# Attention with selected blocks and a window: two factors in one scaling operation

## The reference

```python
ss = jnp.where(dsel >= 0, ss - sl[..., None, None] * dsel, NEG)
ps = jax.nn.softmax(ss.reshape(B, G, R, T, -1), axis=-1).reshape(ss.shape)
o_sel = jnp.einsum('bgrtns,bgtnsd->bgrtd', ps.astype(vb.dtype), vb)
...
pw = jax.nn.softmax(sw, axis=-1)
o_win = jnp.einsum('bgrts,bgsd->bgrtd', pw.astype(vwb.dtype), vwb)
...
gt = jax.nn.sigmoid(gates.reshape(B, S, 3, G, R).transpose(2, 0, 3, 4, 1))[..., None]
o = gt[0] * o_cmp + gt[1] * o_sel + gt[2] * o_win
```

## Time and profile before

| | |
|---|---|
| median of three runs | 3860.39 us (3858.7 to 3864.57) |
| the profiled execution | 3864.79 us, span 3863.0 us |
| mean granted clock of TensorE | 0.946 of 2.4 GHz |
| TensorE (PE) busy in the span | 3528.5 us, 91% |
| VectorE (DVE) busy | 1776.0 us, 46% |
| ScalarE (ACT) busy | 869.9 us, 23% |
| GpSimd (POOL) busy | 1030.7 us, 27% |
| attention stage | 925 to 1290 us from the span's start |

### The profile page before, as it was taken

How to read it: one execution, slowest core, us unless ns; L and a number is a source line. 1 busy time by engine, 2 the same in 40 slices (tenths; PEclk the granted TensorE clock), 3 DMA queues, 4 the chain that set the end, 5 groups by cost and what they waited for, 6 DMA issues and landing times. The chain is left out here.

```text
span 3863.0 us, 55754 instructions
## 1 busy us (share of the span) xinstructions
PE 3528.5 (91%) x23230; PEld 2909.7 (75%) x23230; DVE 1776.0 (46%) x2725; ACT 869.9 (23%) x1260; POOL 1030.7 (27%) x491
## 2 busy tenths in 40 slices
PE   5999999989999898999999889959896899999997
PEld 4878777767777676888888767748784778888886
DVE  4762555423877734555555636134443322223233
ACT  2012122122434203111111220235431121111112
POOL 3332333333210234121212054122212332122221
PEclk7999999998999998999999989969997899999998
DMA  3453334333000312322222046221002111111111
GB/s 92 137 179 116 110 99 118 104 111 102 8 8 1 113 46 89 109 93 69 72 82 76 30 153 150 89 77 36 19 3 93 55 44 44 55 43 54 38 49 44
DMA packets 310711, 290.79 MB, mean 75 GB/s; under 512 B 21454, under 2 KB 276992, under 8 KB 309304
## 3 DMA queue, kind: packets, MB, share of 16 engines
q1 hardware_dynamic: 283738, 205.62, 18.2%
q10 hardware_dynamic: 26482, 82.06, 5.6%
q0 software_dynamic: 288, 0.20, 0.1%
HBM read 224.26 MB, written 63.57 MB: 75 GB/s over the span
## 5 line engine op out<-in xcount | busy, mean ns | idle before, releaser
L713 POOL TENSOR_TENSOR ffn_wlo<-ffn_raw,ffn_whi 128x1024 fp32r<-128x1024 f32 x88 | 211.4, 2404 | 1067.3 <-ACT ffn_whi L901 1012.9
L203 PE MATMUL up<-h_hi,ffn_whi 128*128 128x512 f32 x1408 | 439.6, 394 | 21.3 <-POOL h_lo L404 20.9
L203 PE MATMUL up<-h_lo,ffn_whi 128*128 128x512 f32 x1408 | 436.2, 391 | 0.0
L203 PE MATMUL up<-h_hi,ffn_wlo 128*128 128x512 f32 x1408 | 435.4, 390 | 0.0
L192 POOL TENSOR_TENSOR whi<-raw,ones 128x1024 fp32r<-128x1024 f32 (+1 forms) x83 | 155.3, 1872 | 754.9 <-PE acc L1409 460.9
L203 PEld LDWEIGHTS up<-h_hi,ffn_whi 128*128 128x128 f32 x1408 | 263.4, 189 | 79.2 <-POOL h_lo L404 14.4
L203 PEld LDWEIGHTS up<-h_lo,ffn_whi 128*128 128x128 f32 x1408 | 265.9, 189 | 56.2
L203 PEld LDWEIGHTS up<-h_hi,ffn_wlo 128*128 128x128 f32 x1408 | 265.7, 189 | 56.1
L1409 PE MATMUL acc<-h_hi,whi 128*128 128x512 f32 x816 | 273.6, 417 | 8.3 <-POOL h_lo L404 8.3
L804 DVE TENSOR_TENSOR ffn_prod<-ffn_act,up 128x1024 f32<-128x1024 f32 x44 | 53.8, 1222 | 465.6 <-PE up L203 460.8
L1409 PE MATMUL acc<-h_lo,whi 128*128 128x512 f32 x816 | 256.6, 396 | 0.0
(11 more groups left out here) (549 smaller groups left out, 6635.7 us busy)
## 6 DMA issues: line engine op xcount, KB each, us to landing
raw<-w_in SPq DMA_DIRECT2D x51, 512.0 KB
projT<-proj_stage ACTq DMA_DIRECT2D x51, 512.0 KB, 2.7
ffn_ada_raw<-w_ada SPq DMA_DIRECT2D x24, 1024.0 KB, 5.0
ffn_raw<-w_up SPq DMA_DIRECT2D x44, 512.0 KB
ffn_draw<-w_down SPq DMA_DIRECT2D x11, 1024.0 KB, 6.9
ffn_raw<-ffn_w_gate SPq DMA_DIRECT2D x22, 512.0 KB
ffn_raw<-ffn_w_up SPq DMA_DIRECT2D x22, 512.0 KB
ffn_draw<-ffn_w_down SPq DMA_DIRECT2D x11, 1024.0 KB, 4.7
```

Source lines behind the costliest of these rows:

```text
L203: last = nc.tensor.matmul(acc[:, t, :], w[:, k, w_cols], x[:, k, t * HALF:(t + 1) * HALF], start=(k == 0 and i == 0), stop=(k == k_tiles - ...
L713: nc.gpsimd.tensor_tensor(w_lo[i][:], raw[i][:], w_hi[i][:], ALU.subtract).then_inc(s[f"up_split{i}"], 1)
```

## The change

The product of inverse sum and gate (L2251) is taken out. The scaling (L2254) takes the inverse sum and the gate as its two factors per query, and multiplies by both. The semaphore `weighted`, which counted the products, becomes `inverted` and counts the reciprocals. The column `small[3:4]` is no longer written. All other engines' programs stay.

```diff
@@ nsa_attend
-    names = both("q_in q_split scores_done max_done exp_done weighted scaled grouped group_copied o_done o_read") + ...
+    names = both("q_in q_split scores_done max_done exp_done inverted scaled grouped group_copied o_done o_read") + ...
@@ weight(j)
                 dve.wait_ge(s[f"exp_done{r}"], j // 2 + 1)
                 dve.wait_ge(s[f"scaled{r}"], j // 2)
-                steps.link(nc.vector.reciprocal(small[r][:, 2:3], small[r][:, 1:2]))
+                nc.vector.reciprocal(small[r][:, 2:3], small[r][:, 1:2]).then_inc(s[f"inverted{r}"], 1)
                 gate = (1 + r) * NSA_H + h
-                nc.vector.tensor_tensor(small[r][:, 3:4], small[r][:, 2:3], N["gates"][:, i, gate:gate + 1], ALU.mult).then_inc(s[f"weighted{r}"], 1)
                 n = tiles(i, r) * P
-                dve.wait_ge(s[f"weighted{r}"], j // 2 + 1)
-                nc.vector.tensor_scalar(prob[r][:, 0:n], prob[r][:, 0:n], small[r][:, 3:4], None, ALU.mult).then_inc(s[f"scaled{r}"], 1)
+                dve.wait_ge(s[f"inverted{r}"], j // 2 + 1)
+                nc.vector.tensor_scalar(prob[r][:, 0:n], prob[r][:, 0:n], small[r][:, 2:3], N["gates"][:, i, gate:gate + 1],
+                                        ALU.mult, ALU.mult).then_inc(s[f"scaled{r}"], 1)
```

More of the change, by code:

```diff
@@ L2091, in nsa_attend @@
     raw, w_hi, w_lo = (x[0][:, 0:4, :] for x in mem.weights)
-    names = both("q_in q_split scores_done max_done exp_done weighted scaled grouped group_copied o_done o_read") + "o_in0 o_in1 o_in2 o_in3 o_in4 o_in5 o_in6 o_in7 vector_step pool_step weight_loaded weight_high weight_split"
+    names = both("q_in q_split scores_done max_done exp_done inverted scaled grouped group_copied o_done o_read") + "o_in0 o_in1 o_in2 o_in3 o_in4 o_in5 o_in6 o_in7 vector_step pool_step weight_loaded weight_high weight_split"
     banks = [(f"sc{r}", [P, S], F32) for r in range(2)] + [(f"{n}{r}", [P, HALF], F32) for n in ("pt", "ob") for r in range(2)]
```

## The result

The changed kernel takes 3822.9 us at the median of five runs (3814.8 to 3825.5), against 3864.6 before in the same measurement (3858.7 to 3869.4). The ratio is 0.9894, interval 0.9879 to 0.9909, so some 41 us faster (35 to 47 by the interval). The direction and the places were forecast.

A forecast was written before the change was run, and what follows sets the result against it. In the attention stage, the tensor engine was taken to lose time to waits for DVE's loop and to its lower clock. Terms of 12 (A), 7 (B) and 6 (C) gave 25 us, so 3835 us, range 3826 to 3843, low end 3824.

The forecast's parts named there:

- second factor: In DVE's scaling, the gate as another factor per partition was to cost 0.06 us per scaling.
- fast form: DVE's faster mode for the scaling, expected to stay; the rival that the second factor costs it had chance 0.09, about 3848.
- net 0.14 us per job: DVE's loop: 0.195 us saved by dropping the product, less 0.06 for the longer scaling.
- Term C: Small row blocks: the shorter loop saves 1.0 us per head; 6 us taken in all, bounds 0 and 11.
- Term A: Head boundaries: tensor engine waits behind GpSimd shrink, as one operation queues instead of two; 12 us, bounds 9.5 to 14.1.
- wait for the copy between: Head boundaries: a wait between two short waits, named in the rival that the clock still falls, without a size.
- my replay: One head boundary reworked with one queueing: the first wait goes, 0.4 us of the second wait's 1.34 stays.
- term B: Tensor engine clock at head boundaries: four of five falls to 1.2 GHz go; 7 us, bounds 0 and 8.5.
- Beyond these jobs the loop is ahead, and the saving is idle time of DVE: Jobs past the small row blocks: the shorter loop was to gain nothing there.
- The clock did not keep falling: Rival at head boundaries: shortened waits still drop the tensor engine's clock; 18 us gain at most, about 3844, chance 0.18.
- The waiting was swallowed: Answers a rival: the scaling meets another GpSimd instruction and the tensor engine waits as long as before; 3854, chance 0.09.
- The slower case: Rival: the scaling takes its slow form and still queues behind GpSimd; 8 us or more slower, about 3869, chance 0.04.

The follow-up runs named there:

- e3: Kernel before the change, with GpSimd's query splitting for heads 2 to 7 left out but for two columns of one operation; 3827.5 us, ratio 0.9924.
- e4: Changed kernel with GpSimd's query splitting for heads 2 to 7 left out but for two columns of one operation; 3820.7 us, ratio 0.9898.
- e1: Kernel before the change, its product kept but written as a scaling by a factor per partition, which does not queue behind GpSimd; 3838.6 us, ratio 0.9944.
- e5: Changed kernel with a second, unused reciprocal ahead of the scaling in every job, making the loop longer without queueing; 3841.4 us, ratio 0.9937.
- e9: Kernel before with its product in the non-queueing form, and GpSimd's splits starting only after the widest selected-branch scaling; 3841.0 us, ratio 0.9940.
- e12: Changed kernel with a second reciprocal only in the six jobs of row blocks 5 to 7 of each head; 3832.0 us, ratio 0.9920.
- e8: Changed kernel measured once more, unchanged; 3822.4 us, ratio 0.9886.
- e10: Kernel before the change, with GpSimd's splits starting only after the widest selected-branch scaling; 3838.0 us, ratio 0.9934.
- e7: Changed kernel with the copies of odd groups put ahead of the maximum of job j + 2 on DVE; 3845.7 us, ratio 0.9953.
- e11: Kernel before the change, with the maximum of job j + 2 ahead of product and scaling of job j + 1; 3848.5 us, ratio 0.9960.

## Why the prediction was wrong in size

**The place and the two mechanisms were right.** The 0.06 us of the second factor, the fast form, the net 0.14 us per job, one queueing instead of two: each was measured as said. Term C was to be 1.0 us per head and is 0.94 (e3 to e4, and in the last head).

**Term A was read off the wrong row.** I bounded it by 14.1 us, the waits of PE's matmuls. That row counts from the modelled end of the last matmul, and matmuls overlap: in the changed kernel one of 0.28 us starts at 1162.25 and the next at 1162.37. It also holds only the waits for the scaling. The weight loads' rows come nearer. Before:

```profile
PEld pt L2173 <- DVE att_prob L2254: 20.6, 27, 1.8
...
PEld ob L2190 <- DVE att_probT L2276: 10.9, 22, 0.8
...
PEld pt L2173 <- DVE att_probT L2276: 8.2, 18, 0.6
```

In e3, without GpSimd at the boundaries, these three rows are 5.1, 10.9 and 3.3 us. So the boundaries cost 15.5 us for the scaling and 4.9 for the copies ahead of transposes, 20.4 in all. The lengths of the heads say the same: GpSimd cost 29.3 us, of which 8.5 are the clock and 20.8 the waits. The matmuls' rows for the same two, 13.6 and 1.1, give 14.7. I had 12, with 14.1 as the most. The copies stand behind the scaling in DVE's queue and were late with it: the "wait for the copy between", which I named and did not price. Over the whole stage the three rows fell from 39.7 us to 8.1 + 1.8 + 1.0 = 10.9, by 28.8; with the clock's five stretches, 8.5, and the first one below, 1.7, that is 39.0, and the stage became 37.4 shorter, so the sum is good to a few us.

I also read one boundary for five: my replay leaves 0.4 us of a second wait of 1.34 at each, but the five second waits are 0.27, 1.47, 1.34, 0.17 and 1.34. At the two short ones the clock had already fallen as the first wait ended, at 1014.0 and 1153.8, while term B let the falls hang on the second waits.

**"Beyond these jobs the loop is ahead, and the saving is idle time of DVE"** was the false sentence. Between a head's first row blocks and its last, DVE hardly waits for the tensor engine (0.3 us in e4, nothing in e3), so 0.14 us per job add up to some 1.9 us over 14 jobs. Of these the tensor engine itself has 0.94, term C; the other 0.9 are lead at the head's end (1.11 to 2.05, and 1.51 to 2.40 us, e3 to e4). This is where GpSimd comes, and the lead swallows the wait for it. My replay kept the old lead and left 0.4 us per boundary; e1 and e5, which have one queueing and a loop slightly longer than the old one, show 0.64 and 0.76. Per head the gain of 6.3 us comes apart so: term C is 0.94. The queueing that is gone is worth 46.45 - 43.18 = 3.3 us as measured, and 3.9 without the 0.61 by which e1's own loop is longer. What one queueing still costs without the lead is 43.18 - 0.61 - 41.08 = 1.5 us, and the lead takes it all; e5, e9 and e12 give 1.4 to 1.6 for it in the same way. My replay had 0.4 left at five boundaries, 2 us in all; without the lead it would have been 1.5 at six, 9 us, and with it nothing was left.

**Term B** was 7 us and works out at 8.5, half of five stretches of 3.4: none of the five falls is left, and with one queueing none is left in e1, e5, e9 and e12 either. Of the first stretch at 1.2 GHz, in head 0, which I had left out, 20.5 us became 17.1 in the profiled execution, 1.7 us of time; in e8, the same kernel again, and in e4 and e5 it is 13.7, in the kernel before without splits 20.5. What it hangs on stays open.

**The rivals.** The clock did not keep falling. The fast form was not lost. The waiting was swallowed: the scaling of 128 elements, which now meets GpSimd's later instructions at the start of a head, takes 744 ns in the mean of 16 against 286 before, and no matmul waits for it. The slower case had no part. The low end of my range stood on the bound of 14.1 us, and so the range missed.

## What to carry to other kernels

Where two engines go at nearly the same pace, time saved on the one that is ahead is not idle: it is a buffer, and its worth is read at the next disturbance, so look for what comes later and how long it holds. Count the operations that contend with GpSimd rather than their length; a 0.16 us product cost nearly 4 us per head because it queued. And bound a wait of TensorE by the rows of its weight loads and of all that is queued behind the late instruction.

## What the runs showed of the hardware beyond what was expected

A product on 128x1 elements written on two tensors took up to 2300 ns beside GpSimd; written with the gate as a factor per partition it took 212 to 217 ns in all 128 cases (e1). Without GpSimd beside it the second form is slower, 214 against 160 ns.

The second factor per partition costs the same 0.06 us at every width: 346 ns at 128 elements and 811 at 1024, against 286 and 754.

Waits of 0.40 to 0.76 us at the boundaries (e1, e5, e9, e10, e12) were never followed by a fall of TensorE's clock to 1.2 GHz; in e7 and e11, with waits of up to 1.7 us, it fell at five and at all six of the boundaries.
